# The c norms, the gates' softplus and the taps of the first projections, reordered behind the direct part of a two-block kernel

## The reference, cut to what matters

```python
q = _rmsnorm(c_q, q_norm) @ w_uq
kv = _rmsnorm(c_kv, kv_norm) @ w_ukv
k_pe = _rope(k_pe, cos, sin)
qkv = silu(conv(qkv, w))
q, k = _l2norm(q) * GDN_DK ** -0.5, _l2norm(k)
beta = sigmoid(b_logit)
g = -exp(A_log) * softplus(a_logit + dt_bias)
o = _gated_delta_chunked(q, k, v, beta, g)
```

## Time and profile before

| | us |
|---|---|
| median of three runs | 2768.9 |
| lowest, highest | 2768.87, 2770.62 |
| the profiled execution | 2772.03 |
| its span, first to last instruction | 2770.2 |

### The profile page before, as it was taken

How to read it: one execution, slowest core, us unless ns; L and a number is a source line. 1 busy time by engine, 2 the same in 40 slices (tenths; PEclk the granted TensorE clock), 3 DMA queues, 4 the chain that set the end, 5 groups by cost and what they waited for, 6 DMA issues and landing times.

```text
span 2770.2 us, 41156 instructions
## 1 busy us (share of the span) xinstructions
PE 2695.2 (97%) x16208; PEld 2390.9 (86%) x16208; DVE 1942.5 (70%) x2998; ACT 1308.4 (47%) x2047; POOL 144.1 (5%) x132
## 2 busy tenths in 40 slices
PE   8989999999999999999999999999999999999998
PEld 7778988988899788888888889998888888888887
DVE  6777777778796886556555678997667466575665
ACT  2175544334444554444444554457554444444443
POOL 0000000000002000000000170111100000000000
PEclk9999999999999999999999999999999999999999
DMA  9944245667886786555555555554545555555554
GB/s 386 402 147 159 92 159 185 214 218 270 310 300 229 249 305 206 190 190 185 189 189 190 187 177 169 178 170 135 172 155 181 193 190 192 194 186 195 190 191 144
DMA packets 158162, 565.19 MB, mean 204 GB/s; under 512 B 17553, under 2 KB 21905, under 8 KB 157841
## 3 DMA queue, kind: packets, MB, share of 16 engines
q1 hardware_dynamic: 157968, 562.56, 60.1%
HBM read 560.39 MB, written 2.10 MB: 203 GB/s over the span
## 4 chain that ended last, share of the span: by engine, by line
PE 84%; DVE 8%; DMA 3%; ACT 3%; issue 2%; POOL 0%; SPq 0%; DVEq 0%; ACTq 0%; POOLq 0%
PE BK L363 17%; PE BK L361 17%; PE BK L364 9%; PE BK L360 8%; PE BK L375 4%; PE BK L377 4%; PE BK L376 4%; PE BK L366 4%; PE BK L368 4%; PE BK L367 4%; DVE LO L722 3%; PE BK L473 2%; DVE B L934 2%; DMA EARLY<-wada_dram 1%; PE BK L388 1%
## 5 line engine op out<-in xcount | busy, mean ns | idle before, releaser
L566 ACT ACTIVATE HI<-RAW 128x1024 fp32r<-128x1024 f32 x824 | 873.3, 1060 | 1178.2 <-PE BK L361 645.6
L722 DVE TENSOR_TENSOR LO<-RAW,HI 128x1024 fp32r<-128x1024 f32 x824 | 1011.5, 1228 | 383.9 <-ACT HI L566 381.9
L363 PE MATMUL BK<-H,HI 128*128 128x512 f32 x2160 | 867.9, 404 | 19.5 <-DVE LO L722 19.0
L361 PE MATMUL BK<-H,HI 128*128 128x512 f32 x2128 | 841.0, 397 | 0.0
L364 PE MATMUL BK<-H,LO 128*128 128x256 f32 x2160 | 601.1, 278 | 0.0
L360 PE MATMUL BK<-H,LO 128*128 128x256 f32 x2128 | 595.8, 280 | 0.2 <-DVE H L760 0.2
L360 PEld LDWEIGHTS BK<-H,LO 128*128 128x128 f32 x2128 | 401.2, 189 | 93.5 <-DVE H L760 0.6
L364 PEld LDWEIGHTS BK<-H,LO 128*128 128x128 f32 x2160 | 408.1, 189 | 84.9 <-issue 0.7
L363 PEld LDWEIGHTS BK<-H,HI 128*128 128x128 f32 x2160 | 411.4, 190 | 32.0 <-DVE LO L722 23.3
L361 PEld LDWEIGHTS BK<-H,HI 128*128 128x128 f32 x2128 | 400.9, 188 | 3.9
L366 PE MATMUL BK<-H,HI 128*128 128x256 f32 x1280 | 377.2, 295 | 14.8 <-DVE LO L722 8.0
(11 more groups left out here) (268 smaller groups left out, 2554.6 us busy)
## 6 DMA issues: line engine op xcount, KB each, us to landing
RAW<-wst_dram SPq DMA_DIRECT2D x837, 512.0 KB, 3.4
RAW<-wada_dram SPq DMA_DIRECT2D x155, 512.0 KB, 4.8
EARLY<-wada_dram SPq DMA_DIRECT2D x37, 512.0 KB, 11.0
EARLY<-wst_dram SPq DMA_DIRECT2D x19, 512.0 KB, 12.6
X<-xT_dram SPq DMA_DIRECT2D x8, 512.0 KB, 7.1
B<-bias_dram SPq DMA_DIRECT2D x32, 128.0 KB, 3.4
out_dram<-B SPq DMA_DIRECT2D x4, 512.0 KB, 2.7
B<-gain_dram SPq DMA_DIRECT2D x1, 1024.0 KB, 4.5
```

The lines of the kernel that those rows point to most:

```text
L361: e.matmul(bk[:, :], hh, H[:, k, :], start=False, stop=last, skip_group_check=True).then_inc(S["tile"], 1)
L363: e.matmul(bk[:, :], hh, H[:, k, :], start=first, stop=False, skip_group_check=True)
L566: e.activation(HI[:, u % NHL, :], raw_at(slot), ACT.Copy).then_inc(S["hi"], 1)
L722: e.tensor_tensor(LO[:, u % NHL, :], raw_at(slot), HI[:, u % NHL, :].bitcast(f32), sub).then_inc(S["lo"], 1)
```

## The change

Where `by_v` is set, DVE copies a block instead of ACT (`copy_half`); it is set for every second bank. The squares of a half are one ACT operation over four blocks, written to the free buffers of B2, with no sums on GpSimd; the sums are eight ones-matmuls, emitted after nine turns of the new task `cnorms`. Both roots are taken together into RS[0] and RS[2] with one table preload ahead of the squares. The rows of both halves follow in a task `crows` (first turn two tiles after, gap 3). `scalars` starts at tile 260 with gap 10; its softplus waits for both roots to be emitted, and its beta comes behind, as Tanh(x/2), with a multiply-add in `beta_gate`. `qkv_chain` starts at 268 and waits until softplus is emitted. The key's turn is its own task, 60 tiles later with gap 14.

```diff
@@ -611,7 +611,7 @@
                 q.wait_ge(ready)
-                e.activation(m28(BETA), BA_T.rearrange("p (m h) -> p m h", m=2)[:, :, 0:8], ACT.Sigmoid).then_inc(S["l2_a"], 1)
+                e.activation(m28(BETA), BA_T.rearrange("p (m h) -> p m h", m=2)[:, :, 0:8], ACT.Tanh, scale=0.5).then_inc(S["l2_a"], 1)
 
@@ -795,6 +795,10 @@
 
+            def copy_half(dst, src, done, free):
+                q.wait_ge(done, free)
+                e.tensor_copy(dst, src).then_inc(S["ev_v"], 1)
+
             def rope_half(turned):
@@ -838,8 +842,10 @@
 
-            def beta_gate(grown, beta):
+            def beta_gate(grown, beta, at):
                 q.wait_ge(grown, beta)
+                e.tensor_scalar(BETA, BETA, 0.5, 0.5, mult, add).then_inc(S["l2_v"], 1)
+                q.wait_ge(("l2_v", at + 1))
                 e.tensor_tensor(BG, BG, BETA, mult).then_inc(S["l2_v"], 1)
@@ -1122,8 +1128,11 @@
 
-            def copy_out(dst, bk, tok, own, free=None):
-                a = do("copy_sum", "ev_a", dst, bk[:, 0:256], tok, free)
+            def copy_out(dst, bk, tok, own, free=None, by_v=False):
+                if by_v:
+                    a = do("copy_half", "ev_v", dst, bk[:, 0:256], tok, free)
+                else:
+                    a = do("copy_sum", "ev_a", dst, bk[:, 0:256], tok, free)
                 own[0].release(own[1], a)
@@ -1368,38 +1377,58 @@
             cq_tok = [None] * 8
-            SQS = [Stats(x_stat), None]
+            c_stat = [None, None]
+            roots = []
+            CSQ = B2[:, 0:8, :]
 
...
                 def f(bk, tok, own):
-                    cq_tok[j] = copy_out(CQ[j], bk, tok, own, x_used)
-                    yield
-                    while j > 3 and SQS[0].done is None:
-                        yield
-                    if j == 4:
-                        SQS[1] = Stats(*SQS[0].before, SQS[0].done)
-                    SQS[j // 4].square(CQ[j], cq_tok[j])
-                    if j % 4 == 3:
-                        yield
-                        yield from cnorm(j // 4)
+                    cq_tok[j] = copy_out(CQ[j], bk, tok, own, x_used, by_v=j // 2 % 2 == 1)
+                    yield
                 return f
...
 
-            def cnorm(half):
-                k = yield from SQS[half].finish_steps(512, 1e-6, *([h_tok[15]] if half == 0 else [need(H2_tok, 3)]))
-                name = "q_a_norm" if half == 0 else "kv_a_norm"
-                for j in range(4):
+            def cnorms():
+                while None in cq_tok:
+                    yield
+                do("root_table", "st_a", n=0)
+                sq = [do("square", "st_a", CSQ[:, 4 * half:4 * half + 4, :], X[:, 4 * half:4 * half + 4, :], cq_tok[4 * half:4 * half + 4], h_tok[15]) for half in range(2)]
+                for _ in range(9):
+                    yield
+                c_bk = []
+                for half in range(2):
+                    bi, bk, fr = mbank.get()
+                    for j in range(4):
+                        c_stat[half] = do("stat_add", "st_p", bk, CSQ[:, 4 * half + j, :], j == 0, j == 3, sq[half], fr if j == 0 else None)
+                    c_bk.append((bi, bk))
+                yield
+                steps = [rsqrt_steps(RS[:, 2 * half, :], SQ[:, 1, :] if half else RS[:, 1, :], c_bk[half][1][:, 0:256], 1.0 / 512, 1e-6, c_stat[half], h_tok[15], loaded=True) for half in range(2)]
+                for f in steps:
+                    next(f)
+                yield
+                for half in range(2):
+                    roots.append(whole(steps[half]))
+                    mbank.release(c_bk[half][0], roots[half])
+                yield
+                later(crows(), 2, 3)
+
+            def crows():
+                for j in range(8):
+                    half = j // 4
                     i, t, fr = tv.get()
-                    c = do("scaled", "ev_v", t, CQ[4 * half + j], col(name, j), RS[:, 0, :], mult, mult, k, fr)
-                    yield
-                    H2_tok[4 * half + j] = yield from split(H2, 4 * half + j, t, c, raw_free[NRAW:])
-                    tv.release(i, H2_tok[4 * half + j])
+                    c = do("scaled", "ev_v", t, CQ[j], col("kv_a_norm" if half else "q_a_norm", j % 4), RS[:, 2 * half, :], mult, mult, roots[half], fr)
+                    yield
+                    H2_tok[j] = yield from split(H2, j, t, c, raw_free[NRAW:])
+                    tv.release(i, H2_tok[j])
 
             def ev_kpe(bk, tok, own):
-                k = lin_tok["ba"] = copy_out(BA, bk, tok, own, tk_cos)
-                yield
-                k = yield from rope(KPE, BA, k)
+                lin_tok["ba"] = copy_out(BA, bk, tok, own, tk_cos)
+                yield
+                later(key_rope(), 60, 14)
+
+            def key_rope():
+                k = yield from rope(KPE, BA, lin_tok["ba"])
                 k = do("rope_half", "ev_v", k)
@@ -1413,12 +1442,12 @@
 
-            def ev_qkv(j, wide):
+            def ev_qkv(j, wide, by_v=False):
                 def f(bk, tok, own):
...
                     else:
-                        raw_tok[j] = copy_out(B1[:, j, :], bk, tok, own, x_stat)
+                        raw_tok[j] = copy_out(B1[:, j, :], bk, tok, own, x_stat, by_v=by_v)
                         yield
@@ -1427,6 +1456,8 @@
                 js = [n - 9 for n in ns]
+                while lin_tok["soft"] is None:
+                    yield
                 ahead = None
@@ -1448,9 +1479,11 @@
                 mbank.release(bi, k)
+                k2 = do("softplus_in", "l2_v", k, n=2)
+                while len(roots) < 2:
+                    yield
+                a2 = lin_tok["soft"] = do("softplus", "l2_a", k2, n=3)
                 a1 = do("beta", "l2_a", k)
-                k2 = do("softplus_in", "l2_v", k, n=2)
-                a2 = do("softplus", "l2_a", k2, n=3)
                 yield
@@ -1461,9 +1494,9 @@
                 yield
-                lin_tok["sc"] = do("beta_gate", "l2_v", a, a1)
-
-            lin_tok["sc"] = None
+                lin_tok["sc"] = do("beta_gate", "l2_v", a, a1, n=2)
+
+            lin_tok["sc"] = lin_tok["soft"] = None
             l2_tok = [None, None]
@@ -1648,20 +1681,21 @@
             def ev_first(n):
-                return ev_c(n) if n < 8 else ev_kpe if n == 8 else ev_qkv(n - 9, False)
+                return ev_c(n) if n < 8 else ev_kpe if n == 8 else ev_qkv(n - 9, False, FIRST.index(n) // 2 % 2 == 1)
             for b, n in enumerate(FIRST):
...
                 later(ev_first(n)(bk[:, 256 * (b % 2):256 * (b % 2) + 256], done_tok[b | 1], (own, b % 2)))
-            later(scalars(), 16, 14)
+            later(cnorms(), 0, 1)
+            later(scalars(), 4, 10)
             later(l2norm(0), 64, 6)
-            later(qkv_chain(Q03), 20, TAPS[0])
+            later(qkv_chain(Q03), 12, TAPS[0])
             later(gdn(), 96, HAND)
...
 
-            while None in (cq_tok[7], RN["kpe"], lin_tok["ba"]):
+            while None in (H2_tok[7], RN["kpe"], lin_tok["ba"]):
                 w.force()
-            c_used = [cq_tok[7], RN["kpe"], lin_tok["ba"], *p1_end]
+            c_used = [H2_tok[7], RN["kpe"], lin_tok["ba"], *p1_end]
             pr = Ring(w, [B2[:, 11 + i, :] for i in range(4)], c_used)
@@ -1945,7 +1979,7 @@
             x_tok = [None] * 16
-            ST = Stats(SQS[1].done, *x_free)
+            ST = Stats(c_stat[1], *x_free)
 
```

More of the change, by code:

```diff
@@ L950, in vector @@
                       split_lo=split_lo, tensors=tensors, scaled=scaled, root_half=root_half, root_out=root_out,
-                      stat_product=stat_product, total=total, gain=gain, normed=normed, rope_cos=rope_cos, rope_half=rope_half, rope_sin=rope_sin, taps=taps,
+                      stat_product=stat_product, total=total, gain=gain, normed=normed, rope_cos=rope_cos, rope_half=rope_half, copy_half=copy_half, rope_sin=rope_sin, taps=taps,
                       ba_copy=ba_copy, softplus_in=softplus_in, decay_log=decay_log, cumulated=cumulated, beta_gate=beta_gate,
```

## The result

The changed kernel takes 2776.15 us (median of 8 runs, 2774.87 to 2784.52) beside 2769.29 us for the kernel before in the same call (8 runs, 2768.27 to 2770.71). The ratio is 1.0025, with a 95% interval of 1.0017 to 1.0034: **slower by 6.9 us**, where 2763.6 had been forecast. The profiled execution took 2778.02 us, with a span of 2776.1.

The account below looks back on a forecast made before the run. PE, busy 97%, was taken as the bound, its waits for LO as the gain, with DVE bounding the changed front: unit 47 at 200.9 instead of 206.2 us, so 2768.9 - 5.3 = 2763.6 us, range 2759.0 to 2767.6 (8 in 10).

Parts of the forecast that it names:

- Copies, squares: After the direct part: eight bank copies on DVE, 2.7 us, free; two ACT squares, 1.06 us each, ending PE's 0.7 us wait.
- Additions: Eight ones-matmuls instead of two sums, 0.44 us each: 2.65 us more on PE, all on the path.
- Roots: Both roots taken together keep DVE until 158.7 us; LO36 ends 1.0 us before PE wants it, so no wait.
- Table loads: Three left, softplus's preload paid among them; ACT spends 3.8 instead of 10.3 us on loads.
- First taps: From tile 280: first tap ends at 163.0 us, LO37 is late, PE idles 3.1 us, then loses 1.5 at lower clock.
- From there DVE is the bound: Tiles 280 to 364: DVE needs 9.6 us per 24 tiles against PE's 8.4; unit 47 at 200.9 us, gain 5.3.
- Rival B: Front PE-bound, DVE not late: unit 47 at 193.0 us, gain 13.2, 2755.7 us; chance 0.13 including half that gain.
- What is moved later: Taps 4 tiles later, delta rule 8 tiles later: free, with +-1 us for other meetings with the softmax pipeline.
- Rival D: Slower: the delta rule's 8-tile move adds 15 score-mask waits at tiles 550 to 650, +5.9 us, 2774.8; chance 0.04.

Follow-up runs that it names:

- e7: The changed kernel without softplus's explicit table preload: 2775.61 us, ratio 1.0016 to the kernel before.
- e11: e5 without softplus's preload, c rows' gap 7 not 3, first taps behind LO37, two more catch-up gaps, key's turn at 100 not 60 tiles: 2762.67 us.
- e5: The changed kernel, front untouched, with one tap-chain gap of 3 instead of 5 tiles, so later taps and delta rule keep before's tiles: 2766.28 us.
- e1: The kernel before with the tap chain's first turn at 24 instead of 20 tiles, so the delta rule slips 8 tiles: 2779.08 us, ratio 1.0026.
- e10: The changed kernel with the taps of tile 526 and all later blocks of that chain 12 tiles later, the delta rule unmoved: 2769.05 us, ratio 0.9995.
- e6: The kernel before with only the delta rule's second half 8 tiles later: 2772.39 us, ratio 1.0006.
- e2: The changed kernel with the delta rule another 4 tiles later, taps unmoved: 2779.68 us, ratio 1.0029.
- e4: The kernel before with the delta rule's first half 8 tiles later, the second half following, taps unmoved: 2774.61 us, ratio 1.0010.
- e3: The changed kernel with additions, roots, softplus and first taps 4 tiles earlier, so taps and delta rule keep before's tiles: 2769.46 us, ratio 0.9992.

## Why the prediction was wrong

**What held.** *Copies, squares:* free, as said; the eight copies on DVE took 2.7 us (143.89 to 146.63), as taken. *Additions:* the eight matmuls took 3.62 us, 0.45 each (0.44 taken). *Roots:* no wait. *Table loads:* three left; the explicit preload is paid, and e7 prices it. The Trainium skill's drain behind a load (ScalarE: Activation LUTs, What ACT_TABLE_LOAD costs, about 1.38 us) was weighed ahead of the result; behind the loads at 158.41 and 160.29 the next activation starts 0.02 and 0.01 us after their end, so this trace shows none either. *First taps:* the tap ended at 162.21 (forecast 163.0), and PE idled 3.21 us (forecast 3.1), at the lower clock afterwards, as said: 0.50 in the window of 165 to 170 us. The whole sequence stood 0.7 to 1 us earlier since the direct part ended at 145.2 us, and not at 146.2.

*From there DVE is the bound:* right, with its sizes a little off. The LOs came at the listed times, less the 1 us of the earlier start (LO38 and LO44 on DVE; they end at 169.5 and 189.9, listed 170.4 and 190.9):

```profile
168.33 1.22 DVE L722 TENSOR_TENSOR LO<-RAW,HI 128x1024 fp32r<-128x1024 f32 x1
...
188.72 1.22 DVE L722 TENSOR_TENSOR LO<-RAW,HI 128x1024 fp32r<-128x1024 f32 x1
```

PE's waits behind them were three, between 186 and 194 us, of 0.91 us in all, where five of 3.3 us had been listed: PE came to them later than listed, having run slower behind the long wait than the 1.5 us taken: unit 37 took 5.92 us (166.01 to 171.93), two small matmuls of the gates in it, where 2.80 and 1.5 had been put (the granted clock reads 0.50 from 165 to 170 us; and before's unit 38, which the 1.5 was read from, took 4.46 us, not 4.3). With DVE the bound, the end is the same: 5.2 us ahead at unit 47, counted from LO32, against 5.3. That the number is this close is in part luck: 2.4 us less of small waits stand against the longer slow stretch. Rival B, the front PE-bound (-13.2), did not come; e11, which comes nearest, had 10.3 us at unit 47.

**The step that failed** is the one headed *What is moved later*: "free, with +-1 us for other meetings with the softmax pipeline". It checked the far deadline (which tile first asks for the rule's second half) and not the near neighbours, and the sum took both kernels to run at the same rate from tile 376 on. The two moves cost 12.0 us between unit 60 and the end (from -5.1 to +6.9): 7.3 us up to unit 92, the waits of 5.2, 2.25 and 1.5 us and the slow clock behind the first two among them; 3.1 more up to unit 152, the wait near unit 128 among them; 1.7 behind unit 282, less 0.1 between. e5 brings 4.3 us home with the same front and without the moves; e1 loses 7.5 with the moves alone. It is shown, then, that the moves are the cause, and by e10 that the place of the taps from tile 526 on holds a large part of it.

Rival D had the right agent, the rule's 8 tiles, and a wrong place and price: it looked at the score masks of tiles 550 to 650, for 15 waits of 0.75 us. The largest piece came as one wait at tile 536, at the join of two block shapes, where a bank is wanted from a half-sum. It could have been found beforehand: the emission order from tile 516 to 536 is in the code, and before's trace holds ACT's idle 4.36 us in front of that very Tanh. The forecast followed LO one by one up to unit 47 and asked of the rest only whether it had the same rate.

**What stays open.** The wait near unit 128 comes with a second half that is 8 tiles late (e6), but its size and the clock fall vary where DVE's order is the same; e6's 1.8 us in the time are inside its interval of no change. The last 1.7 us come where the order is the same as before's. The kernels with both moves lose 0.9 to 1.7 us there (changed kernel again, e1, e2, e7), the others between -1.0 and +0.7; whether that is a remnant in the engines' phase or varying clock falls was not tried. Some profiled executions, which the table shows, stand off their medians: e4's 3.7 us above, e5's 2.2 above, e3's 3.2 below.

## To carry to other kernels

A change that lets a side task start a few tiles later moves all that follows it. So list the emission order, old and new, at each later join where block shapes or phases change, and ask of every engine what stands behind the first instruction that must wait; a deadline hundreds of tiles away says nothing about this. Where only the front is to be improved, win back the shift right behind it, so that everything downstream keeps its old order (e5: one gap of 3 instead of 5 tiles turned +6.9 into -4.3). And measure the progress at the stage that was changed as well as the total: the front was right to 0.2 us while the kernel as a whole had the other sign.

## What the runs showed of the hardware

The explicit preload of a table set that is active costs the full 1.28 us, and its removal gave 1.45 us at unit 47 (e7). The granted clock does not fall at the same places in every execution of one order: between units 60 and 92, e5 lost 1.5 us to one at 316 to 319 us, behind the same two waits of 0.8 us that before has without a fall, and the runs of one kernel spread over 2.4 us (before) to 9.7 us (the changed kernel) in the call of the result. So one profiled execution can't show a difference of 2 us in the total, though the sum to one unit can: up to unit 60 two profiles of the changed kernel differ by 0.06 us.
